# Softmax weights left unnormalised: 64 columns of ones beside the high values, outputs scaled at the end

## What is computed

```python
s = jnp.einsum('bqhd,bkhd->bhqk', qi, k) * scale      # + (li - lk_t) in group B
s = jnp.where(mask[None, None], s, -jnp.inf)
p = jax.nn.softmax(s, axis=-1)
return jnp.einsum('bhqk,bkhd->bqhd', p, v)            # 1024 rows, 8 heads, v 64 wide
```

## Time and profile before

| | us |
|---|---|
| median of 3 runs (lowest, highest) | 2621.74 (2621.46, 2623.41) |
| time of the profiled execution | 2621.32 |
| its span, first to last instruction | 2619.5 |
| group A's part of the span | about 1106 to 1316 |
| group B's part of the span | about 1460 to 1697 |
| mean granted clock of PE, whole span | 0.954 of full speed |

### The profile page before, as it was taken

One profiled execution on the slowest core, in us unless ns is written; L12 is line 12 of the kernel. 1 busy time (PEld: TensorE's weight loads), 2 busy tenths in 40 slices (PEclk: granted clock), 3 DMA queues, 4 the chain that ended last, 5 costly groups with the idle time before them and its releaser, 6 DMA issues. The chain is left out here.

```text
span 2619.5 us, 41638 instructions
## 1 busy us (share of the span) xinstructions
PE 2389.8 (91%) x14715; PEld 2122.8 (81%) x14715; DVE 1541.6 (59%) x2582; ACT 996.2 (38%) x2013; POOL 990.9 (38%) x743
## 2 busy tenths in 40 slices
PE   5999999999989998988889777797899999999985
PEld 4999999988867788867666555585899999998864
DVE  7766666655596223365543555565866666664565
ACT  7222222233353112466533365534422222233443
POOL 1544444434460000065621366422544444434452
PEclk9999999999999999998899787898999999999998
DMA  4444444367573220100054200133344444446664
GB/s 149 137 147 134 150 131 149 117 226 240 175 245 125 96 99 7 44 3 1 1 218 158 82 1 1 49 105 105 99 133 147 133 151 139 155 164 227 199 200 145
DMA packets 244229, 326.67 MB, mean 125 GB/s; under 512 B 31857, under 2 KB 138481, under 8 KB 242065
## 3 DMA queue, kind: packets, MB, share of 16 engines
q1 hardware_dynamic: 244112, 325.20, 37.9%
HBM read 230.31 MB, written 94.69 MB: 124 GB/s over the span
## 5 line engine op out<-in xcount | busy, mean ns | idle before, releaser
L62 PE MATMUL ffn_bank<-x_hi,ffn_w_w_hi 128*128 128x256 f32 (+1 forms) x2464 | 735.2, 298 | 25.8 <-DVE x_lo L969 25.2
L63 PE MATMUL ffn_bank<-x_lo,ffn_w_w_hi 128*128 128x256 f32 (+1 forms) x2464 | 732.9, 297 | 0.0
L64 PE MATMUL ffn_bank<-x_hi,ffn_w_w_lo 128*128 128x256 f32 (+1 forms) x2464 | 732.7, 297 | 0.0
L62 PEld LDWEIGHTS ffn_bank<-x_hi,ffn_w_w_hi 128*128 128x128 f32 x2464 | 471.2, 191 | 28.5 <-DVE x_lo L969 27.6
L63 PEld LDWEIGHTS ffn_bank<-x_lo,ffn_w_w_hi 128*128 128x128 f32 x2464 | 471.6, 191 | 0.0
L64 PEld LDWEIGHTS ffn_bank<-x_hi,ffn_w_w_lo 128*128 128x128 f32 x2464 | 471.2, 191 | 0.0
L738 POOL TENSOR_TENSOR ffn_split_dn_lo<-ffn_in_dn_raw,ffn_split_dn_hi 128x512 fp32r<-128x512 f32 x176 | 250.2, 1426 | 286.7 <-ACT ffn_split_dn_hi L805 281.4
L724 POOL TENSOR_TENSOR ffn_w_w_lo<-gu_raw,ffn_w_w_hi 128x512 fp32r<-128x512 f32 x176 | 240.3, 1367 | 299.1 <-ACT ffn_w_w_hi L755 299.0
L1001 DVE TENSOR_TENSOR ffn_split_a_lo<-ffn_in_a_raw,ffn_split_a_hi 128x512 fp32r<-128x512 f32 (+2 forms) x176 | 218.5, 1257 | 172.7 <-ACT ffn_split_a_hi L807 172.6
L724 POOL TENSOR_TENSOR ffn_w_w_lo<-ffn_w_s,ffn_w_w_hi 128x512 fp32r<-128x512 f32 x132 | 193.0, 1464 | 298.3 <-ACT ffn_w_w_hi L755 298.3
L62 PE MATMUL ffn_bank<-ffn_split_dn_hi,ffn_split_a_hi 128*128 128x512 f32 x704 | 279.2, 397 | 18.2 <-DVE ffn_split_a_lo L1001 16.1
(11 more groups left out here) (424 smaller groups left out, 4305.2 us busy)
## 6 DMA issues: line engine op xcount, KB each, us to landing
gu_raw<-in_w_ffn_gu SPq DMA_DIRECT2D x88, 512.0 KB, 5.2
ffn_w_w_raw<-in_w_ffn_down SPq DMA_DIRECT2D x22, 1024.0 KB, 5.0
a_rows<-ffn_w_a_st SPq DMA_DIRECT2D x44, 512.0 KB, 2.9
t_rows<-ffn_w_w_raw SPq DMA_DIRECT2D x88, 256.0 KB, 2.4
s_rows<-ffn_w_a_st SPq DMA_DIRECT2D x88, 256.0 KB, 2.3
ffn_in_dn_raw<-in_w_ffn_down SPq DMA_DIRECT2D x88, 256.0 KB, 3.8
ffn_in_dn_raw<-t_rows SPq DMA_DIRECT2D x88, 256.0 KB, 3.5
ffn_in_a_raw<-s_rows SPq DMA_DIRECT2D x88, 256.0 KB, 3.2
```

What stands on the lines that cost most here:

```text
L62: pe.matmul(out, w_hi, x_hi, start=first, stop=False)
L63: pe.matmul(out, w_hi, x_lo, start=False, stop=False)
L64: return pe.matmul(out, w_lo, x_hi, start=False, stop=last)
```

## The change

Both groups are changed in the same way.

- The weights `p` are no longer normalised. The exponential no longer accumulates the row sum, and `normalise` of `p` and the one-column reciprocals are gone. `flip_row(g)` waits for `exped`, the exponential itself.
- The high values stand in a tile `v_one` of twice the width, whose other 64 columns are ones, set once by a memset on POOL. The value matmuls with `v_one` fill all 128 partitions of the output bank: 64 with the unnormalised output, 64 with the row sum, the same in each. The matmul with `v_lo` fills the first 64 alone. The order of the three becomes high*high, low value*high weight, high value*low weight.
- `take` is replaced by three instructions for each output half: `copy_out` on ACT into `o_raw` [64, 512], `invert` on DVE, a reciprocal of the 64 partitions of row sums out of PSUM into `inverse` [64, 512], and `normalise` on POOL, their product into `acc`. Each stands at the step at which `take` stood (t = 0 and 4), on DVE behind everything else of that step. There is one `o_raw` and one `inverse`, so each waits for the product before (`o_taken`). A bank is free again after `o_copied` and `inverted`.
- The low values are made at t = 3 in both groups.
- The first piece of `w_out` alone is loaded early, the other seven late, because `v_lo` now lies where the second piece was.

The diff for group B; group A's is the same but for names, and keeps its place for the low values:

```diff
                 def flip_row(g):
-                    pe.wait_ge(normed, g + 1)
+                    pe.wait_ge(exped, g + 1)
...
                             if h:
                                 if n:
-                                    pe.wait_ge(o_taken, 2 * n)
+                                    pe.wait_ge(o_copied, 2 * n)
+                                    pe.wait_ge(inverted, 2 * n)
...
-                        dst = out_of[h][:, c0:HALF]
+                        final = c == HT * (h + 1) - 1
                         high, low = pT_hi[h][:, c, c0:HALF], pT_lo[h][:, c, c0:HALF]
-                        pe.matmul(dst, v_hi[b][:, c, :], high, start=(c == 0), stop=False)
-                        pe.matmul(dst, v_hi[b][:, c, :], low, start=False, stop=False)
-                        last = pe.matmul(dst, v_lo[b][:, c, :], high, start=False, stop=(c == HT * (h + 1) - 1))
+                        pe.matmul(out_of[h][:, c0:HALF], v_one[b][:, c, :], high, start=(c == 0), stop=False)
+                        pe.matmul(out_of[h][0:VD, c0:HALF], v_lo[b][:, c, :], high, start=False, stop=False)
+                        last = pe.matmul(out_of[h][:, c0:HALF], v_one[b][:, c, :], low, start=False, stop=final)
...
-                    act.activation(p[:, g % NP_ROWS, 0:cols], scores[:, g % 2, 0:cols], ACT.Exp, bias=nmax[:, g:g + 1], accum_out=total[:, g:g + 1]).then_inc(exped, 1)
+                    act.activation(p[:, g % NP_ROWS, 0:cols], scores[:, g % 2, 0:cols], ACT.Exp, bias=nmax[:, g:g + 1]).then_inc(exped, 1)
...
-                def take(n, h):
+                def copy_out(n, h):
                     act.wait_ge(pv_ok, 2 * n + h + 1)
+                    if n or h:
+                        act.wait_ge(o_taken, 2 * n + h)
+                    act.activation(o_raw[:, :], out_of[h][0:VD, :], ACT.Copy).then_inc(o_copied, 1)
...
-                def invert(g):
-                    dve.wait_ge(exped, g + 1)
-                    dve.reciprocal(inverse[:, g:g + 1], total[:, g:g + 1]).then_inc(inverted, 1)
+                def invert(n, h):
+                    dve.wait_ge(pv_ok, 2 * n + h + 1)
+                    if n or h:
+                        dve.wait_ge(o_taken, 2 * n + h)
+                    dve.reciprocal(inverse[:, :], out_of[h][VD:P, :]).then_inc(inverted, 1)
...
-                    if g + LEAD < ROWS:
-                        invert(g + LEAD)
+                        if n and t == EARLY_OUT_STEP:
+                            invert(n - 1, 0)
+                        if n and t == LATE_OUT_STEP:
+                            invert(n - 1, 1)
+                for h in range(HALVES):
+                    invert(H - 1, h)
...
+                def normalise(n, h):
+                    pool.wait_ge(o_copied, 2 * n + h + 1)
+                    pool.wait_ge(inverted, 2 * n + h + 1)
+                    pool.tensor_tensor(acc[n % 2 * VD:n % 2 * VD + VD, h * HT:h * HT + HT, HALF + n // 2 * P:HALF + n // 2 * P + P], o_raw[:, :].rearrange("p (t n) -> p t n", n=P),
+                                       inverse[:, :].rearrange("p (t n) -> p t n", n=P), ALU.mult).then_inc(o_taken, 1)
+                    pool.wait_ge(o_taken, 2 * n + h + 1)
...
+                for b in range(2):
+                    pool.memset(plain(v_one[b][:, :, VD:2 * VD]), 1.0).then_inc(ones_in, 1)
+                pool.wait_ge(ones_in, 2)
                 for r in range(PREP):
                     double(0, r)
-                for g in range(-LEAD, ROWS):
+                for g in range(ROWS):
                     n, t = divmod(g, PT)
-                    if g >= 0 and n + 1 < H and t in PREP_STEP:
-                        pool.wait_ge(normed, g + LEAD)
+                    if n and t == EARLY_OUT_STEP:
+                        normalise(n - 1, 0)
+                    if n + 1 < H and t in PREP_STEP:
                         double(n + 1, PREP_STEP[t])
-                    if g + LEAD < ROWS:
-                        normalise(g + LEAD)
-                    if g >= 0 and t == V_STEP + 2:
+                    if n and t == LATE_OUT_STEP:
+                        normalise(n - 1, 1)
+                    if t == V_STEP:
                         v_low(n)
+                        pool.wait_ge(v_lo_ok, n + 1)
...
-W_FIRST = (0, 1)
+W_FIRST = (0,)
```

More of the change, by code:

```diff
@@ L1471, in mla_prompt @@
         late_hi, late_lo = [k.sb(f"late_{n}", [P, PT, HALF], F32R) for n in ("hi", "lo")]
-        v_hi, v_lo = [[k.sb(f"v_{n}{b}", [P, PT, VD], F32R) for b in range(2)] for n in ("hi", "lo")]
-        nmax, total, inverse = [k.sb(n, [P, ROWS]) for n in ("nmax", "total", "inverse")]
+        v_one = [k.sb(f"v_one{b}", [P, PT, 2 * VD], F32R) for b in range(2)]
+        v_lo = [k.sb(f"v_lo{b}", [P, PT, VD], F32R) for b in range(2)]
+        o_raw, inverse = [k.sb(n, [VD, HALF]) for n in ("o_raw", "inverse")]
+        nmax = k.sb("nmax", [P, ROWS])
         assert nc.sbuf_base <= limit
@@ L1757, in fox_prompt @@
         late_hi, late_lo = [k.sb(f"late_{n}", [P, PT, HALF], F32R) for n in ("hi", "lo")]
-        v_hi, v_lo = v_parts
-        nmax, total, inverse = [k.sb(n, [P, ROWS]) for n in ("nmax", "total", "inverse")]
+        v_one, v_lo, inverse = v_parts
+        o_raw = k.sb("o_raw", [VD, HALF])
+        nmax = k.sb("nmax", [P, ROWS])
         scores = k.ps("scores", [P, 2, SEQ])
@@ L1764, in fox_prompt @@
         pT_hi, pT_lo = (early_hi[:, :, :], late_hi[:, :, :]), (early_lo[:, :, :], late_lo[:, :, :])
-        out_of = (turn[0:VD, :], out[0:VD, :])
+        out_of = (turn, out)
         turned, hi_ok, lo_ok, doubled = k.sem("turned"), k.sem("hi_ok"), k.sem("lo_ok"), k.sem("doubled")
@@ L1871, in values @@
                         c0 = max(0, c - HT * h) * P
-                        dst = out_of[h][:, c0:HALF]
+                        final = c == HT * (h + 1) - 1
                         high, low = pT_hi[h][:, c, c0:HALF], pT_lo[h][:, c, c0:HALF]
-                        pe.matmul(dst, v_hi[b][:, c, :], high, start=(c == 0), stop=False)
-                        pe.matmul(dst, v_hi[b][:, c, :], low, start=False, stop=False)
-                        last = pe.matmul(dst, v_lo[b][:, c, :], high, start=False, stop=(c == HT * (h + 1) - 1))
-                        if c == HT * (h + 1) - 1:
+                        pe.matmul(out_of[h][:, c0:HALF], v_one[b][:, c, :], high, start=(c == 0), stop=False)
+                        pe.matmul(out_of[h][0:VD, c0:HALF], v_lo[b][:, c, :], high, start=False, stop=False)
+                        last = pe.matmul(out_of[h][:, c0:HALF], v_one[b][:, c, :], low, start=False, stop=final)
+                        if final:
                             last.then_inc(pv_ok, 1)
@@ L1927, in v_high, with copy_out @@
                         act.wait_ge(loaded[1], 16)
[L1928 to L1930 removed]
+                    act.activation(v_one[n % 2][:, :, 0:VD], v_rows(n), ACT.Copy).then_inc(v_hi_ok, 1)
+                def copy_out(n, h):
                     act.wait_ge(pv_ok, 2 * n + h + 1)
[L1932 removed]
+                    if n or h:
+                        act.wait_ge(o_taken, 2 * n + h)
+                    act.activation(o_raw[:, :], out_of[h][0:VD, :], ACT.Copy).then_inc(o_copied, 1)
                 for hf in range(HALVES):
```

111 lines of the change are left out of this document (62 added, 49 removed).

## The result

The changed kernel takes 2653.99 us (median of 4, 2650.99 to 2655.96) against 2621.6 (2621.37 to 2623.41): ratio 1.0121, 95% interval 1.0104 to 1.0139. It is slower by 32 us where the forecast said 22 us faster. The profiled execution took 2655.96 us. Over its whole span the granted clock is 0.956, where before it was 0.954, so the clock over the whole program does not account for the loss.

The account below looks back on a forecast made before the run. TensorE, busy 91% of the span, was taken as the bound, with stalls behind POOL's normalisation and `v_lo`. The terms -3.2 - 21.4 - 6 + 5 + 4 = -21.6 took 2621.3 to 2600 us; range 2575 to 2685.

Parts of the forecast that it names:

- the 0.98 us margin at flip 6: In group A, the DVE and ACT chain's low 5 is half done just 0.98 us before the flip of row 6.
- part 2: Two 64x512 reciprocals a head on DVE, steps 0 and 4; DVE's wait replaces POOL's at flip 6: -3.2 us.
- Rival 2: At TensorE's waits for POOL: no new wait forms and all of them go, 2558 us or lower; chance 0.04.
- X: Price of one 64x512 reciprocal on DVE, bounded by 0.7 and 5.8 us and taken as 1.2 us.
- rival 1: DVE, steps 4 and 0: the reciprocal is dear, 2641 us at 2.7 us each, 2747 at 5.8; chance 0.42.
- The break-even of 2.1: On DVE, a reciprocal of about 2.1 us, where its cost at both steps and the ends uses up the 22 us.
- Part 3: `v_lo` made on POOL at step 3: group B's second stall goes whole, -21.4 us.
- part 4: TensorE's clock in group B: without its second stall B should look like A, -6 us; A's clock stays.
- Parts 1: Normalisations leave POOL, accumulator reads ACT, one-column reciprocals DVE; outside the stall they cost nothing beside TensorE's work.
- part 5: Wider stationary operands in the value matmuls with `v_one`, 128 columns instead of 64: 0.3 us a head, +5 us.
- part 6: Ends of both groups: a reciprocal and a POOL multiply replace one copy behind the last value matmul, +4 us.
- rivals 2 and 3: The third: DVE and ACT set rows 1 to 3 of B, half the gain is lost, 2611 us; chance 0.08.

Follow-up runs that it names:

- the copy: Changed kernel with the 64x512 reciprocal replaced by a copy, so outputs are multiplied by the row sums instead of divided: 2583.86 us, ratio 0.9857.
- the ladder: Kernel before with reciprocals and multiplies of 1 to 128 columns added on DVE at its start; only its rows were read, not its time.
- the half reciprocal: Changed kernel with the reciprocal over 256 of the 512 columns and a copy of the other 256: 2619.87 us, ratio 0.9992.
- the earlier `v_lo` alone: Kernel before with group B's low values made on POOL at step 4 instead of step 5, nothing else: 2596.07 us, ratio 0.9902.
- reciprocal at step 0 alone: Changed kernel with the reciprocal kept at step 0 and a copy in its place at step 4: 2606.43 us, ratio 0.9935.
- step 4 alone: Changed kernel with the reciprocal kept at step 4 and a copy in its place at step 0: 2635.66 us, ratio 1.0045.

## Why the prediction was wrong, point by point

- **What bounds the kernel, and the 0.98 us margin at flip 6: right.** With the copy the flip waits for low 5 in place of POOL (20.7 and 24.6 us against 22.7 and 28.0), the "one wait takes the place of another" of part 2. At a copy's price that part gives 0.7 us a head, and a head of A became 0.8 shorter (24.7 to 23.9). Rival 2, in which no new wait forms, is refuted by the same rows.
- **Part 2, X = 1.2 us: the step that failed.** It is 3.36. The step was "The extra is therefore mostly paid once per instruction": the ladder shows it paid by every column, 6.3 ns each. "3 ns more than the one-column one", carried over 510 columns, gave 1.7 at most, and the middle of 0.7 and 1.7 was then taken without a reason of its own. The bounds, 0.7 and 5.8, held the price; the choice within them rested on 3 ns between two instructions of different stages, where one and the same shape differs by 10 ns and more between stages (154 and 164, 154 and 167). The Trainium skill, "VectorE: DVE Perf Modes", section "First, the fixed hardware budget", was set aside because of that 3 ns. The direction that the forecast drew from the page is borne out. The page names a repeat count of 8 and no price; read as eight times the 1.04 ns of an ordinary column it is too high, since the slope measured is six times that. The estimate from it, 4.4 us, was still nearer to 3.36 than mine.
- **The formula of rival 1: right.** At X = 3.36 it adds 2.16 at step 4 and 1.56 at step 0. The waits grew by 2.7 at each flip 6 for the 2.67 between copy and reciprocal, and the preparation waits 1.47. What I had wrong is the count: 16 of each. Head 0 of a group has no output at step 4 and its last head no preparation, so there are 14 and 12. 14 x 2.16 + 12 x 1.56 + 4 for the ends = 53, and 2600 + 53 = 2653 against a median of 2654. That is closer than its terms deserve, as the next two points show. The break-even of 2.1 was met by the half reciprocal, 2.12 us at a ratio of 0.9992.
- **Part 3, -21.4, and part 4, -6: right for the earlier `v_lo` alone.** It gave 25.5 us against their 27.4; the waits for `v_lo` went whole (0.2 of 21.4 us are left), so 4 or so came with the clock, where 6 had been expected. B's clock went to 0.92, above the 0.90 expected. In the change itself B has 0.86 over the stretch of the earlier trace rows: most of the gain in clock is not there, which rival 1 had not priced (some 8 to 9 us, as far as the remainders above can be put down to it).
- **Parts 1, 5 and 6: no error that the runs can tell.** The sum with a copy's price, 2591, was measured at 2584, so in sum the forecast is 7 us too dear there; errors that cancel among the parts are not excluded. Of part 5's two wider steps a piece one shows in the head above: the matmul out of `v_one` still follows the one out of `v_lo` after 0.06 us, and is itself followed after 0.12, where the last of the three in the kernel before is followed after 0.06 (1186.52 to 1186.58):

```profile
1195.09 0.22 PE L1585 MATMUL mla_turn<-mla_early,mla_v_lo 128*64 128x128 f32 x1
1195.15 0.28 PE L1586 MATMUL mla_turn<-mla_early,mla_v_one 128*128 128x128 f32 x1
1195.27 0.39 PE L62 MATMUL mla_scores<-mla_kT_hi,mla_qT_hi 96*128 96x384 f32 x1
```

  The end of group A, behind its last value matmul, is part 6: 3.36 + 1.26 in place of one copy.

```profile
1340.72 0.28 PE L1586 MATMUL mla_out<-mla_late_lo,mla_v_one 128*128 128x128 f32 x1
...
1341.06 3.36 DVE L1700 RECIPROCAL mla_inverse<-mla_out 64x512 f32<-64x512 f32 x1 [1.56 <-PE mla_out L1586]
1344.59 1.26 POOL L1728 TENSOR_TENSOR all_acc<-mla_o_raw,mla_inverse 64x512 f32<-64x512 f32 x1 [3.63 <-DVE mla_inverse L1700]
```

- **The gain was small from the start, and I saw only half of why.** Of the 38 us that the change gains without its reciprocal, 25 can be had in the kernel before by one moved instruction. What the idea itself, no normalisation of the weights, adds to that is 12 (good to about 6) at a copy's price for the reciprocal, and the reciprocal costs 70.
- **The chances do not add up.** 0.46 with rivals 2 and 3 is 0.58, not 0.53, beside rival 1's 0.42; the forecast gives 0.53, 0.06 and 0.41. The 0.47 for no gain or a loss was near even, so the miss of the sign is no surprise by its own account.
- **Left open.** Some 8 us of the 70 are put down to the clock by the stretches of three runs, not by a run that changes the clock alone. No other way to the same quotient than a reciprocal and a product was measured.

## What to carry to other kernels

Before work is moved off a late engine, look for the second releaser of the wait it is late for: where another engine is within a microsecond, that microsecond is about all there is to gain at that wait, and what is put on that engine ahead of the wait is paid in full. Fewer instructions on more columns is a good trade only if the operation's price per column is known near that width; a slope taken from its two smallest shapes is none. Where the bounds of a price lie far apart and the sign of the sum hangs on it, compare the difference that chooses between them with what the same shape varies by in the same trace: here 3 ns against 10 and more.

## What the runs showed of the hardware

- DVE's reciprocal costs 6.3 ns a column in fp32 (943 ns at 128, 1760 at 256, 3360 at 512), five times a copy's 1.3 ((694 - 356) / 256), out of PSUM on 64 partitions as out of SBUF on 128; 64 x 128 out of SBUF takes 924 ns.
- The shortest instructions of one shape differ between places of a program: the reciprocal of one column took 154 and 164 ns, that of two 154 and 167 in the kernel before.
- DVE's multiply by a value per partition takes 753 ns for 1024 columns, 686 for 896 and 620 for 768 when POOL is not making `v_lo`. Beside `v_lo` (1.28 us) 768 columns took 1.47 us and 896 took 1.77. Which shape is slow changes with the step of `v_lo`, 768 in A (step 3) and 896 in B (step 4), and in the last head of each group the multiply takes its short time: in A `v_lo` starts 0.37 us after it, in B `v_lo` is over before it starts. So it is the two side by side that costs. The Trainium skill, "GPSIMD Engine Reference", section "1. Specifications", says that GpSimd shares its memory interfaces with VectorE, with contention when VectorE runs in a mode that uses two ports or reads two inputs from SBUF. The trace agrees that they contend; which of the two cases this is it does not show.
- The granted clock of a stretch does not follow from its longest stall. In the same work of A (1145 to 1270 us) one stall of 2.5 us a head went with 0.90 and 0.92 (before, and before with the earlier `v_lo`, which leaves A as it is) and one of 2.8 with 0.92 (copy); 2.8 with a second one of 1.5 went with 0.96 (reciprocal at step 0 alone), 5.5 alone with 0.86 (step 4 alone), and 5.5 with 1.5 with 0.90 (the change).
